# Sums and empty products in the waits of two norms and of the first token turns, the first weight unit in halves, and one gating at the end of a four-layer decoder stack

## What is computed

```
h = x
for i in range(2):
    h = h + 0.5 * swiglu(rmsnorm(h, norm_ffn1[i]), ffn1_w_in[i], ffn1_w_out[i])
    hn = rmsnorm(h, norm_mix[i])
    h = h + (short_conv_mixer(hn, ...) if i == 0 else dilated_attention_mixer(hn, ...))
    h = h + 0.5 * swiglu(rmsnorm(h, norm_ffn2[i]), ffn2_w_in[i], ffn2_w_out[i])

mod = silu(c) @ mod_w + mod_b
shift_m, scale_m, gate_m, shift_f, scale_f, gate_f = split(mod, 6)
xm = rmsnorm(h, norm_mix_w) * (1.0 + scale_m) + shift_m
h = h + gate_m * hybrid_mixer(xm, ...)
xf = rmsnorm(h, norm_ffn_w) * (1.0 + scale_f) + shift_f
h = h + gate_f * hierarchical_moe(xf, ...)
return rmsnorm(h, norm_out_w)
```

## Time and profile before

| what | value |
|---|---|
| median of 3 runs | 1887.58 us |
| the three runs | 1878.91, 1887.58, 1887.96 us |
| profiled execution | 1887.4 us |
| its span (first to last instruction) | 1885.2 us |
| mean granted clock of the tensor engine | 0.988 |
| tensor engine busy | 1849.6 us, 98% |
| vector, scalar engine busy | 1220.2 us, 943.4 us |
| data moved | 379.16 MB, 201 GB/s |

### The profile page before, as it was taken

The page is one execution under the profiler, slowest core; times in us unless marked ns, Lnnn a source line. Parts: engine busy times, 40 slices in busy tenths (PEclk is TensorE's granted clock), DMA queues, the critical chain, the costliest instruction groups (busy, mean ns, idle before and its releaser), DMA issues.

```text
span 1885.2 us, 24482 instructions
## 1 busy us (share of the span) xinstructions
PE 1849.6 (98%) x9398; PEld 1529.7 (81%) x9398; DVE 1220.2 (65%) x1308; ACT 943.4 (50%) x1037; POOL 117.4 (6%) x142
## 2 busy tenths in 40 slices
PE   8999999999999999999999999999999999999997
PEld 6888998888888888888888888898988788876764
DVE  4566666566644557665556566787655766868677
ACT  5443435344544355544445434564445455667574
POOL 0100000000000000000100000223100050000000
PEclk9999899999999999999999999999999999999998
DMA  6877455777555547555644777544233357879695
GB/s 232 292 250 244 144 187 170 235 260 249 169 170 189 186 159 215 179 179 179 90 73 160 246 244 260 170 157 146 101 119 136 111 209 249 324 247 343 248 337 188
DMA packets 239272, 379.16 MB, mean 201 GB/s; under 512 B 13511, under 2 KB 149069, under 8 KB 239184
## 3 DMA queue, kind: packets, MB, share of 16 engines
q1 hardware_dynamic: 233728, 365.13, 57.0%
q0 software_dynamic: 5456, 12.81, 4.0%
HBM read 372.83 MB, written 10.30 MB: 203 GB/s over the span
## 4 chain that ended last, share of the span: by engine, by line
PE 93%; DVE 4%; ACT 1%; DMA 1%; issue 0%; SPq 0%; POOLq 0%; ACTq 0%; DVEq 0%
PE ps L374 27%; PE ps L376 27%; PE ps L375 27%; PE ps L1057 2%; PE ps L1079 1%; PE ps L2790 1%; PE ps L761 1%; PE ps L1067 1%; DVE lo L357 1%; PE ps L1548 1%; PE ps L1035 1%; ACT hi L351 0%; PE ps L1563 0%; PE ps L2837 0%; PE ps L488 0%; PE ps L811 0%
## 5 line engine op out<-in xcount | busy, mean ns | idle before, releaser
L357 DVE TENSOR_TENSOR lo<-raw,hi 128x2048 fp32r<-128x2048 f32 x296 | 679.1, 2299 | 323.2 <-ACT hi L351 322.2
L351 ACT ACTIVATE hi<-raw 128x2048 fp32r<-128x2048 f32 x296 | 565.3, 1915 | 370.0 <-PE ps L376 361.7
L374 PE MATMUL ps<-hi,xT_hi 128*128 128x512 f32 x1376 | 549.9, 400 | 8.1 <-DVE lo L357 5.6
L376 PE MATMUL ps<-hi,xT_lo 128*128 128x512 f32 x1376 | 538.2, 391 | 0.0
L375 PE MATMUL ps<-lo,xT_hi 128*128 128x512 f32 x1376 | 538.2, 391 | 0.0
L374 PEld LDWEIGHTS ps<-hi,xT_hi 128*128 128x128 f32 x1376 | 259.8, 189 | 62.1 <-DVE lo L357 6.1
L376 PEld LDWEIGHTS ps<-hi,xT_lo 128*128 128x128 f32 x1376 | 259.4, 188 | 56.0
L375 PEld LDWEIGHTS ps<-lo,xT_hi 128*128 128x128 f32 x1376 | 259.9, 189 | 49.4
L374 PE MATMUL ps<-hi,ffn_hhi 128*128 128x512 f32 x352 | 137.8, 391 | 0.0
L375 PE MATMUL ps<-lo,ffn_hhi 128*128 128x512 f32 x352 | 137.1, 389 | 0.0
L376 PE MATMUL ps<-hi,ffn_hlo 128*128 128x512 f32 x352 | 137.0, 389 | 0.0
(11 more groups left out here) (453 smaller groups left out, 2248.1 us busy)
## 6 DMA issues: line engine op xcount, KB each, us to landing
raw<-in_ffn_w_in SPq DMA_DIRECT2D x176, 512.0 KB, 4.5
raw<-in_ffn_w_out SPq DMA_DIRECT2D x88, 512.0 KB, 4.1
raw<-in_attn_w_qkv SPq DMA_DIRECT2D x72, 512.0 KB, 4.5
raw<-in_w_in SPq DMA_DIRECT2D x64, 512.0 KB, 4.3
modraw<-in_mod_w SPq DMA_DIRECT2D x48, 512.0 KB, 6.7
raw<-in_w_gate SPq DMA_DIRECT2D x48, 512.0 KB, 4.3
raw<-in_w_up SPq DMA_DIRECT2D x48, 512.0 KB, 5.4
raw<-in_w_down SPq DMA_DIRECT2D x48, 512.0 KB, 4.5
```

Of the source, the lines that this page charges most:

```text
L351: nc.scalar.activation(hi[u % SPLIT][:, :], raw[raw_slot(u)][:, :], ACT.Copy).then_inc(S("hi_ready"), 1)
L357: nc.vector.tensor_tensor(lo[u % SPLIT][:, :], raw[raw_slot(u)][:, :], hi[u % SPLIT][:, :].bitcast(F32), ALU.subtract).then_inc(S("lo_read ...
L374: nc.tensor.matmul(dst, w_hi, x_hi, start=start, stop=False, skip_group_check=True)
L376: return nc.tensor.matmul(dst, w_lo, x_hi, start=False, stop=stop, skip_group_check=True)
```

## The change

Five edits, and two that only merge semaphores (`gd_ld` into `gd_small`, two new counters shared by two pairs of steps each):

1. The first unit is loaded, rounded, split and waited for in two halves of 128x1024. Its rounding and splitting come between the second and the third block of the first token turns, not after the fourth. Units 1 and 2 stay behind the fourth block.
2. Empty products: 5 ahead of the first block's turn, and 7, 5, 2 and 6 behind the four blocks.
3. At the norm before the convolution: 11 sums and 3 empty products ahead of the turns, 2 sums between the two tiles' turns, 3 sums behind.
4. `turn_norm` has 4 empty products between the two tiles' turns by default, which is so at the norm before the experts. At the norm before the mixer there is none between, but 8 behind, once the first two pieces are copied out.
5. At the end each tile's two parts (`y_back` and PSUM) are added before one multiplication with the gate row.

```diff
+        def first_unit_act(act):
+            act.wait_ge(S("first_half_loaded"), 32)
+            nc.scalar.activation(hi[0][:, 0:UNIT // 2], raw[0][:, 0:UNIT // 2], ACT.Copy).then_inc(S("first_half_hi"), 1)
+            act.wait_ge(S("raw_loaded0"), 32)
+            nc.scalar.activation(hi[0][:, UNIT // 2:UNIT], raw[0][:, UNIT // 2:UNIT], ACT.Copy).then_inc(S("hi_ready"), 1)
...
-        def warm(n, bank):
+        def warm(n, bank, c=0):
             for _ in range(n):
-                nc.tensor.matmul(ps[:, bank, 0:P], ones[:, :], ones[:, :], start=True, stop=True, skip_group_check=True)
+                nc.tensor.matmul(ps[:, bank, c:c + P], ones[:, :], ones[:, :], start=True, stop=True, skip_group_check=True)
...
-            pe_wait_unit(pe, u, it, per)
+            if u:
+                pe_wait_unit(pe, u, it, per)
+            else:
+                pe.wait_ge(S("first_half_lo"), 1)
...
+                if u == 0 and (t, k) == (0, 2):
+                    pe_wait_unit(pe, u, it, per)
...
+                if n == 0 and i == 1:
+                    first_unit_act(act)
...
+                if u == 0:
+                    for k in range(2):
+                        for g in range(2):
+                            sp.dma_start(dst[:, 2 * k:2 * k + 2, g, :], in_src(i, it, half, g)[:, 2 * k:2 * k + 2, :]).then_inc(
+                                S("raw_loaded0" if k else "first_half_loaded"), 16)
+                    return
...
-        def mod_cols_pe(pe, n, vecs=(0, 1)):
+        def mod_cols_pe(pe, n, vecs=(0, 1), ks=range(KT)):
...
-                for k in range(KT):
+                for k in ks:
...
             for t in range(TT):
                 dve.wait_ge(S(f"y_loaded{t}"), 32)
                 then(nc.vector.tensor_tensor(y_back[:, t, 0, :], y_back[:, t, 0, :], y_back[:, t, 1, :], ALU.add))
+            for t in range(TT):
+                wait_acc(dve, DNU[0][1], t)
+                for c in range(2):
+                    y = y_back[:, t, 0, c * 512:c * 512 + 512]
+                    nc.vector.tensor_tensor(y, y, ps[:, 2 * t + c, :], ALU.add).then_inc(S("gated"), 1)
+                dve.wait_ge(S("gated"), 4 + 2 * t + 2)
                 then(nc.vector.tensor_tensor(y_back[:, t, 0, :], y_back[:, t, 0, :], gate_row[:, 1, :], ALU.mult))
-                then(nc.vector.tensor_tensor(h[:, t, :], h[:, t, :], y_back[:, t, 0, :], ALU.add))
+                nc.vector.tensor_tensor(h[:, t, :], h[:, t, :], y_back[:, t, 0, :], ALU.add).then_inc(S("h_ready"), 2)
...
-            add_gated(dve, DNU[0][1], 1, ysb_all, 1, (0, 1, 2, 3))
...
-            for half, t in TILE_PARTS:
+            warm(5, 0)
+            for (half, t), bridge in zip(TILE_PARTS, (7, 5, 2, 6)):
                 turn_tile(pe, 0, t, half)
+                warm(bridge, 0)
...
-            turn_norm(1, 1, then=lambda: mod_cols_pe(pe, 0, (1,)), ahead=lambda: mod_cols_pe(pe, 0, (0,)))
+            turn_norm(1, 1, ahead=lambda: (mod_cols_pe(pe, 0, (0,)), mod_cols_pe(pe, 0, (1,), range(0, 3)), warm(3, 3, 256)),
+                      between=lambda: mod_cols_pe(pe, 0, (1,), range(3, 5)), then=lambda: mod_cols_pe(pe, 0, (1,), range(5, 8)))
...
-            turn_norm(6, 7, then=lambda: None, ahead=lambda: gates_pe(pe))
+            gates_pe(pe)
+            turn_pe(pe, 7, xn, "norm_x", (X_AT[6] + 1, X_AT[6] + 2))
+            pe.wait_ge(S("turned_val"), KT * 7 + 2)
+            warm(8, mix_bank(0))
```

More of the change, by code:

```diff
@@ L104, in build @@
                            ("gd_s", 1), ("gd_out0", 1), ("ret_out0", 1), ("gd_ws", 1), ("gd_out1", 1), ("ret_out1", 1)),
+            "first_scalar": (("first_half_hi", 1), ("cs_ready", 1)),
+            "first_vector": (("first_half_lo", 1), ("conv_pad", 1)),
             "moe_vector": (("rt_gx", 1), ("rt_sx", 1), ("chosen", 2), ("order_ready", 1), ("rank_read", 1), ("slot_ready", 2), ("xtok_lo", 4),
@@ L344, in round_unit @@
         def round_unit(act, u, it=None, per=0):
-            if it is None and ("a", u) in done:
+            if it is None and (u == 0 or ("a", u) in done):
                 return
@@ L353, in split_unit @@
         def split_unit(dve, u, it=None, per=0):
-            if it is None and ("s", u) in done:
+            if it is None and (u == 0 or ("s", u) in done):
                 return
@@ L357, in split_unit, with first_unit_dve @@
             nc.vector.tensor_tensor(lo[u % SPLIT][:, :], raw[raw_slot(u)][:, :], hi[u % SPLIT][:, :].bitcast(F32),
+                                    ALU.subtract).then_inc(S("lo_ready"), 1)
+        def first_unit_act(act):
[3 more added lines that the diff above has]
+            nc.scalar.activation(hi[0][:, UNIT // 2:UNIT], raw[0][:, UNIT // 2:UNIT], ACT.Copy).then_inc(S("hi_ready"), 1)
+        def first_unit_dve(dve):
+            dve.wait_ge(S("first_half_hi"), 1)
+            nc.vector.tensor_tensor(lo[0][:, 0:UNIT // 2], raw[0][:, 0:UNIT // 2], hi[0][:, 0:UNIT // 2].bitcast(F32),
+                                    ALU.subtract).then_inc(S("first_half_lo"), 1)
+            dve.wait_ge(S("hi_ready"), 1)
+            nc.vector.tensor_tensor(lo[0][:, UNIT // 2:UNIT], raw[0][:, UNIT // 2:UNIT], hi[0][:, UNIT // 2:UNIT].bitcast(F32),
                                     ALU.subtract).then_inc(S("lo_ready"), 1)
@@ L544, in build, with turn_pe @@
         TURN_BANK = {n: 0 if n == 5 else 4 for n in (1, 5, 7, 8)}
-        def turn_pe(pe, n, src, ready, counts):
+        def turn_pe(pe, n, src, ready, counts, between=None):
             for t in range(TT):
+                if t and between:
+                    between()
                 pe.wait_ge(S(ready), AT.get(ready, 0) + counts[t])
@@ L812, in mod_cols_pe @@
                                             start=(v == 0 and k == 0), stop=True, skip_group_check=True)
-            if vecs[-1]:
+            if vecs[-1] and ks[-1] == KT - 1:
                 last.then_inc(S("mod_turned"), 1)
@@ L929, in conv_dve @@
             nc.vector.memset(vpad[:, :, 0:2], 0.0).then_inc(S("conv_pad"), 1)
-            dve.wait_ge(S("conv_pad"), 1)
+            dve.wait_ge(S("conv_pad"), AT["conv_pad"] + 1)
             def mix(i):
@@ L2011, in gdn_dve @@
                 nc.vector.tensor_tensor(th(GX)[:, t, :], ps[:, 6, T + t * 8:T + t * 8 + 4], row(DTB, 4), ALU.add).then_inc(S("gd_x"), 1)
+        DECAY_STEPS = 22
         def gdn_decay_pool(pool):
@@ L2034, in gdn_decay_pool @@
             then(nc.gpsimd.tensor_tensor(row(SP_), row(LNP), row(RELU), ALU.add))
+            assert steps[0] == DECAY_STEPS
             for t in range(TT):
-                nc.gpsimd.tensor_tensor(th(LD)[:, t, :], th(SP_)[:, t, :], row(NEA, 4), ALU.mult).then_inc(S("gd_ld"), 1)
+                nc.gpsimd.tensor_tensor(th(LD)[:, t, :], th(SP_)[:, t, :], row(NEA, 4), ALU.mult).then_inc(S("gd_small"), 1)
         def gdn_rec_dve(dve):
@@ L2049, in gdn_decay_dve @@
         def gdn_decay_dve(dve):
-            dve.wait_ge(S("gd_ld"), 2)
+            dve.wait_ge(S("gd_small"), DECAY_STEPS + TT)
             nc.vector.tensor_copy(ldB[:, :, :, :].rearrange("p t h n -> p (t h) n"), spread(row(LD), P)).then_inc(S("gd_ldb"), 1)
@@ L3035, in _ @@
                 tile_dve(dve, 0, half, t, cols[:, COL["ffn1"]:COL["ffn1"] + KT])
-            split_ahead(dve, U0["ffn0"], (0, 1, 2))
+                if (half, t) == (0, 1):
+                    first_unit_dve(dve)
+            split_ahead(dve, U0["ffn0"], (1, 2))
             rstd_dve(dve, 0)
-            dve.wait_ge(S("cs_ready"), 1)
+            dve.wait_ge(S("cs_ready"), AT["cs_ready"] + 1)
             ffn_dve(dve, F0, mod_raw, mod_part, mod_acc, 0, beside_second=bias_dve)
@@ L3080, in _, with turn_norm @@
             nc.tensor.transpose(ps[:, 3, 0:ROWS_B], rows_b[0:ROWS_B, :], ident[0:ROWS_B, 0:ROWS_B]).then_inc(S("tables_turned"), 1)
-            def turn_norm(n, k, then=lambda: warm(BRIDGE_TURN, 3), ahead=lambda: warm(BRIDGE_NORM, 3)):
+            def turn_norm(n, k, then=lambda: warm(BRIDGE_TURN, 3), ahead=lambda: warm(BRIDGE_NORM, 3), between=lambda: warm(4, 3)):
                 ahead()
-                turn_pe(pe, k, xn, "norm_x", (X_AT[n] + 1, X_AT[n] + 2))
+                turn_pe(pe, k, xn, "norm_x", (X_AT[n] + 1, X_AT[n] + 2), between)
                 then()
-            for half, t in TILE_PARTS:
+            warm(5, 0)
+            for (half, t), bridge in zip(TILE_PARTS, (7, 5, 2, 6)):
                 turn_tile(pe, 0, t, half)
+                warm(bridge, 0)
             ffn_pe(pe, F0, after_first=bias_pe)
```

2 lines of the change are left out of this document (1 added, 1 removed).

## The result

| | kernel before | changed kernel |
|---|---|---|
| median of the runs beside each other | 1880.09 us (1877.70 to 1887.96, 6 runs) | 1872.88 us (1871.21 to 1875.85, 6 runs) |
| profiled execution: time, span | 1887.4, 1885.2 us | 1875.31, 1873.3 us |
| its mean granted clock of TensorE | 0.988 | 0.993 |

The account below looks back on a forecast made before the run. The tensor engine, busy 98% of the span, was taken as the bound. Terms -5.1 - 2.6 - 1.0 + 0.3 - 2.45 = -10.85 us took 1887.4 to a forecast of 1876.5 us, range 1870 to 1883.5.

Parts of the forecast that it names:

- Rival 3: Whole kernel: gain doesn't show, low-clock stretches differ between executions; sum only -5.0 us, time 1882.4; chance 0.13.
- A: First token turns and first unit: halves and empty products start products earlier at full clock; -5.1 us.
- B: Norm before the convolution: reordered sums and three empties start the convolution 1.95 us earlier; -2.6 us taken.
- Held by empties and no longer by data: Start: the first product begins at 13.7 us, when the empty products end, its data being ready before.
- the forecast's case: Norm before the convolution: -2.6 us, near the middle between full clock (-4.3) and low clock (-0.7); whole forecast's chance 0.50.
- rival 1: Norm before the convolution: clock stays low through B, worth only -0.7 us, time 1878.4; chance 0.24.
- the sums stood in front of it for 2.3 us: Norm before the convolution: operand ready at 211.67 us, first product only at 213.95, the sums delaying it.
- the argument about turns that I set against B: Norm before the convolution: by the skill's rule transposes don't count as activity, making B -0.7 us; the trace seemed to disagree.
- C: Norm before the mixer: eight empties hold the first product by 0.35 us but keep the clock up; together -1.0 us.
- D: Norm before the experts: four empties between the tokens' turns make token 1's turns 0.3 us later; nothing won.
- E: Kernel's end: summing two parts before one gating saves one 1.26 us vector step per token; -2.45 us.
- Rival 4: After the first units: slower, stretches at full clock fall; from eight new ones gain gone, 1888.0 us or more; chance 0.03.

Follow-up runs that it names:

- halves alone: Kernel before with only the first unit loaded, rounded and split in halves, no empty products; median 1877.26 us against 1882.28, ratio 0.9974.
- empties alone: Kernel before with only the start's 25 empty products, first unit rounded and split whole; median 1886.92 us against 1882.28, ratio 1.0015.
- B alone: Kernel before with only the sums split 11, 2 and 3 and three empties at the norm before the convolution; 1878.17 us against 1882.28, ratio 0.9988.

## Why the prediction came out as it did

The range held the time, and the direction is right, but the sum of 10.85 us describes neither pair of numbers: it is 1.3 less than the 12.1 between the two profiled executions and 3.6 more than the 7.2 between the medians (1.7 more than the 9.2 by the ratio).

- **The basis** was the step that failed. I made the sum against one execution at 1887.4 and took it as typical, 0.2 below the median of three. With more runs the kernel before has medians of 1878.95 to 1882.28, and of its 78 runs of under 1900 us beside the experiments only 14 had a mean granted clock as low as this execution's 0.988. So the starting value was 7.3 too high against the median of 1880.09, and that the gain came out 3.6 too large hid half of it: that the forecast landed within 3.6 us is in part luck. The profiled execution had 34.1 us at the low clock, as much as any of the 14; its three places behind 1200 (mixer and experts) were low there and at full clock in five of the others. Rival 3 named this and got 0.13: it was right that executions differ, and wrong that the gain would then shrink to 5.0, since A removes and B shortens stretches that fell in every execution with the old code.
- **A**, predicted -5.1 (first product 13.7, end 24.8), measured 13.03, 24.26, -5.6. The half roundings took 1.07 and the half splits 1.22, near the estimates of 0.98 and 1.15; turns and empties overlap, so that 3 turns and 13 empties took 4.1 (8.90 to 13.03), less than their sum of 4.6. Both halves of the mechanism are shown: halves alone -4.2, empties alone 0. "Held by empties and no longer by data" is shown, 0.37 us.
- **B**, predicted -2.6 between -4.3 and -0.7. The trace won 3.4 between the first sum and the point in the convolution where the clock is up in both traces. With B alone the best end was reached: 2.0 earlier, and 26 products at 0.12 instead of 0.21 give 2.4 more, at a clock of 1.00 from 204 to 216. Neither the forecast's case (clock up) nor rival 1 (low through) came as such: a short stretch over the turns. The step "the sums stood in front of it for 2.3 us" was wrong in its cause: at the full clock they do not. And the argument about turns that I set against B was decided too soon: the 8 us at 1.00 in the earlier trace rows hold 24 records of empties ahead of the turns, so they show neither that turns hold the clock nor that they don't, and no run here separates the two.
- **Not predicted:** 1.6 us less behind the last sums and 1.6 more at the attention's end. The former are narrow products too, which the one-column reading should have told me; the latter came in 3 of 14 executions.
- **C**, predicted -1.0, measured -1.0 between these two traces, but that is luck, one draw of each; over the nine and five executions it is worth nothing. The empties hold the first product by 0.5, not 0.35.
- **D**, predicted +0.3, measured 0.0: the scaling of token 1 was already as late as the empties.
- **E**, predicted -2.45. The work shrank by just that (12.7 to 10.2), the time by 2.0: the transfers landed later and the first add began after 0.97 us of idling instead of 0.47.
- **Rival 4** did not happen: the new stretch was one, not eight.

The terms of the trace: -5.6 (A) - 3.4 (B) - 1.6 + 1.6 (not predicted) - 1.0 (C) + 0.0 (D) + 0.2 (in the experts) - 2.0 (E) = -11.8, against 11.9 between the spans.

## What to carry to other kernels

Before adding up an edit against one profiled execution, compare its mean granted clock with that of the other runs: here the execution shown had lost about 17 us to the low clock, as much as any of 14, and a sum made against it promises more than the runs can give. A place that falls in every execution is worth an edit; one that falls in one of three is worth a third of its price, less the filler's own cost. And where the clock falls behind a stretch that looks fully busy, look at how wide its products are before moving them: here, widening 32 products cost 0.1 us for each 16 of their records, and on the kernel before it did about as much as the reordering.

## What the runs showed of the hardware that I had not expected

- One-column products took as long as 128-column ones (16 records: 1.84 and 1.95 us) and count as busy in the profile, yet the granted clock fell to 0.50 in or behind them in 19 of 22 cases (two places, eleven executions), and in none of 6 with 128 columns.
- In the changed kernel with wide sums the turns at the norm before the convolution stood between wide sums and wide empties at a clock of 1.00 throughout (199 to 212), as turns behind empties did in the earlier trace rows.
- Between runs of one program the time follows the mean granted clock: 1877.2 to 1878.1 us at 0.993, 1887.1 to 1888.1 at 0.987 (kernel before, 33 runs).
- In the experts' part, which no edit touches, the same two places were low in 8 of 14 executions, up in 5, and one of them low in one: from the first pick product to the last it takes 257.1 us (changed kernel: 257.3) or 254.0.
